# Second block of a two-block transformer kernel: the order of the input chunks, the convolution's taps and head 0's scores

## The reference, cut to what matters

```
fx, cqx, ckvx, krx, gx = split(modulate(rms_norm(x)) @ w_in[l])
q  = rms_norm(cqx, q_norm_g) @ w_uq                 # 8 heads, 64 + 32 rotated
kv = rms_norm(ckvx, kv_norm_g) @ w_ukv              # 8 heads, 64 keys + 64 values
attn = softmax((qn kn + rope(qr) rope(kr)) * scale) @ v      # keys: context and tokens
u = a * sigmoid(g)                                  # a, g: the halves of gx
u = conv(u, w_dw) + b_dw                            # depthwise, 31 taps along the tokens
y_c = silu(layer_norm(u)) @ w_pw2
y_f = Re(fft2(fx)) @ w_fourier
x = x + gate * (concat(y_f, attn, y_c) @ w_o)       # then a feed-forward part
```

## Time and profile before

| what | value |
|---|---|
| median of three runs | 3596.69 us |
| the profiled execution | 3599.15 us, span 3597.4 us |
| PE busy in the span | 3484.3 us (97%) |
| DVE busy | 1746.7 us (49%) |
| ACT busy | 1376.2 us (38%) |
| mean granted PE clock | 0.996 |

### The profile page before, as it was taken

The page is one execution under the profiler, slowest core; times in us unless marked ns, Lnnn a source line. Parts: engine busy times, 40 slices in busy tenths (PEclk is TensorE's granted clock), DMA queues, the critical chain, the costliest instruction groups (busy, mean ns, idle before and its releaser), DMA issues.

```text
span 3597.4 us, 46920 instructions
## 1 busy us (share of the span) xinstructions
PE 3484.3 (97%) x17777; PEld 2703.5 (75%) x17777; DVE 1746.7 (49%) x2536; ACT 1376.2 (38%) x2048; POOL 6.2 (0%) x13
## 2 busy tenths in 40 slices
PE   8999999999999989999999899899999999999999
PEld 5565788777775656887777776588888886579998
DVE  6674434443366754344333557543333356843334
ACT  5553323322245643233222334533323334443334
POOL 0000000000000000000000000000000000000000
PEclk9999999999999999999999999999999999999999
DMA  4121233555541212335565320022222222023332
GB/s 128 51 66 50 79 94 100 152 151 142 156 106 54 63 52 76 94 110 138 161 177 145 94 60 4 2 59 60 64 64 63 60 78 68 4 59 91 91 93 88
DMA packets 577230, 310.26 MB, mean 86 GB/s; under 512 B 28400, under 2 KB 569024, under 8 KB 577088
## 3 DMA queue, kind: packets, MB, share of 16 engines
q1 hardware_dynamic: 576816, 308.18, 30.3%
q10 hardware_dynamic: 272, 0.13, 0.0%
HBM read 297.26 MB, written 2.10 MB: 83 GB/s over the span
## 4 chain that ended last, share of the span: by engine, by line
PE 90%; DVE 4%; ACT 3%; issue 2%; DMA 1%; SPq 0%; DVEq 0%; ACTq 0%
PE ps L1129 14%; PE ps L1130 14%; PE ps L1131 14%; PE ps L1438 10%; PE ps L1440 10%; PE ps L1442 10%; PE ps L1319 2%; PE ps L1638 2%; PE ps L1288 2%; PE ps L1300 1%; PE ps L1213 1%; PE ps L1573 1%; PE ps L1316 1%; PE ps L1294 1%; DVE cacc L2963 1%
## 5 line engine op out<-in xcount | busy, mean ns | idle before, releaser
L1799 ACT ACTIVATE whi<-wraw 128x1024 fp32r<-128x1024 f32 x448 | 470.8, 1052 | 554.4 <-DMA wraw<-in_w_mlp 246.7
L1129 PE MATMUL ps<-uhi,whi 128*128 128x512 f32 (+1 forms) x1456 | 613.1, 421 | 12.4 <-DVE ulo L2454 5.3
L2437 DVE TENSOR_TENSOR wlo<-wraw,whi 128x1024 fp32r<-128x1024 f32 x448 | 545.9, 1219 | 106.6 <-ACT whi L1799 102.0
L1130 PE MATMUL ps<-ulo,whi 128*128 128x512 f32 (+1 forms) x1456 | 572.3, 393 | 0.0
L1131 PE MATMUL ps<-uhi,wlo 128*128 128x512 f32 (+1 forms) x1456 | 572.0, 393 | 0.0
L1129 PEld LDWEIGHTS ps<-uhi,whi 128*128 128x128 f32 x1456 | 274.0, 188 | 102.9 <-issue 38.5
L1130 PEld LDWEIGHTS ps<-ulo,whi 128*128 128x128 f32 x1456 | 274.4, 188 | 72.2 <-issue 16.3
L1131 PEld LDWEIGHTS ps<-uhi,wlo 128*128 128x128 f32 x1456 | 273.6, 188 | 65.2
L1438 PE MATMUL ps<-u2hi,whi 128*128 128x512 f32 (+1 forms) x1216 | 295.7, 320 | 3.6 <-DVE wlo L2437 2.4
L1438 PE MATMUL ps<-yhi,whi 128*128 128x512 f32 (+1 forms) x976 | 295.9, 353 | 0.0
L1440 PE MATMUL ps<-ylo,whi 128*128 128x512 f32 (+1 forms) x976 | 295.0, 353 | 0.0
(11 more groups left out here) (335 smaller groups left out, 4527.2 us busy)
## 6 DMA issues: line engine op xcount, KB each, us to landing
wraw<-in_w_in SPq DMA_DIRECT2D x128, 512.0 KB, 3.8
wraw<-in_w_mlp SPq DMA_DIRECT2D x128, 512.0 KB, 4.0
mod_raw<-in_w_mod SPq DMA_DIRECT2D x96, 512.0 KB, 5.2
wraw<-in_w_mlp_in SPq DMA_DIRECT2D x64, 512.0 KB, 4.3
wraw<-in_w_mlp_out SPq DMA_DIRECT2D x64, 512.0 KB, 3.9
wraw<-in_w_branch SPq DMA_DIRECT2D x16, 512.0 KB, 3.4
wraw<-in_w_out SPq DMA_DIRECT2D x16, 512.0 KB, 3.8
wraw<-in_w_o SPq DMA_DIRECT2D x16, 512.0 KB, 3.8
```

The lines of the kernel that those rows point to most:

```text
L1129: pe.matmul(bank, whs[:, i], x_hi[:, k], start=(i == 0), stop=False)
L1130: pe.matmul(bank, whs[:, i], x_lo[:, k], start=False, stop=False)
L1799: act.activation(whi[:, r], wraw[:, r], ACT.Copy).then_inc(w_hi, 1)
L2437: dve.tensor_tensor(wlo[:, r], wraw[:, r], whi[:, r].bitcast(F32), ALU.subtract).then_inc(w_split, 1)
```

## The change

Only the hand-written list ahead of the loop over heads changes, and with it the place of two rotations in SP's queue. The new list puts both conv and both conv_gate chunks in front of the q chunks. 30 of the 62 taps of the first layer and 19 of the second stand among the input chunks and head 0's first steps (13 and 10 before). The q norm comes behind the first fourier chunk, directly followed by head 0's queries. Head 0's scores alternate with the values and head 1's keys, and the second fourier chunk stands ahead of them all.

```diff
--- before.py
+++ after.py
@@ -354,18 +354,18 @@
     kv = Step("rank_norm", what="kv", tiles=1, width=ALL)
     q = Step("rank_norm", what="q", tiles=2, width=width)
     taps = [Step("tap", slot=t, tap=i) for t in range(2) for i in range(TAPS)]
-    shares = [4, 4, 2] if last else [5, 5, 3]
-    order = [chunk("kv", IN_KV), Step("rank_square", norm=kv), chunk("kr", IN_KR), kv, chunk("q", IN_Q), Step("key_rotate"),
-             chunk("q", IN_Q + P, 1), Step("rank_square", norm=q), chunk("conv", IN_CONV), q, Step("head_key", h=0),
-             Step("key_rest", h=0, width=ALL), chunk("conv_gate", IN_GATE), query(0), *taps[:shares[0]], chunk("conv", IN_CONV + P, 1), rotate(0),
-             *taps[shares[0]:sum(shares[:2])], chunk("conv_gate", IN_GATE + P, 1),
-             Step("query_round", h=0, width=width), query(1), *taps[sum(shares[:2]):sum(shares)], chunk("fourier", IN_FOURIER),
-             *scores(0, 0, 1, 2),
-             rotate(1), chunk("fourier", IN_FOURIER + P, 1), *scores(0, *range(3, a_units)),
-             Step("values", index=0), Step("head_key", h=1), Step("query_round", h=1, width=width),
-             Step("key_rest", h=1, width=ALL), Step("mla_column", h=0, width=width), Step("values", index=1), Step("values", index=2),
-             Step("mla_row", h=0, width=width)]
-    taps = taps[sum(shares):]
+    shares = [0, 4, 8, 12, 16, 18, 19] if last else [0, 6, 12, 18, 23, 27, 30]
+    early = [taps[lo:hi] for lo, hi in zip(shares, shares[1:])]
+    order = [chunk("kv", IN_KV), Step("rank_square", norm=kv), chunk("kr", IN_KR), kv, chunk("conv", IN_CONV),
+             Step("key_rotate"), chunk("conv_gate", IN_GATE), Step("head_key", h=0), Step("key_rest", h=0, width=ALL),
+             chunk("conv", IN_CONV + P, 1), *early[0], chunk("conv_gate", IN_GATE + P, 1), *early[1], chunk("q", IN_Q),
+             *early[2], chunk("q", IN_Q + P, 1), Step("rank_square", norm=q), *early[3], chunk("fourier", IN_FOURIER),
+             q, query(0), rotate(0), *early[4], chunk("fourier", IN_FOURIER + P, 1), Step("query_round", h=0, width=width),
+             query(1), *early[5], *scores(0, 0), Step("values", index=0), *scores(0, 1), rotate(1),
+             Step("values", index=1), *scores(0, 2), Step("head_key", h=1), *scores(0, 3), Step("key_rest", h=1, width=ALL),
+             Step("values", index=2), *scores(0, *range(4, a_units)), Step("query_round", h=1, width=width),
+             Step("mla_column", h=0, width=width), Step("mla_row", h=0, width=width)]
+    taps = taps[shares[-1]:]
     fill = {0: [Step("fourier_features", index=i) for i in range(2 if last else 3)],
             1: [Step("fourier_positions", index=0, width=width)], 2: [Step("fourier_positions", index=1, width=width)],
             3: [Step("fourier_map", index=t, width=width) for t in range(2)]}
@@ -1068,11 +1068,10 @@
                     for to, start in ((64, 80), (80, 64)):
                         sp.dma_start(sq2[to:to + 16, 1, 0:SEQ], sq2[start:start + 16, 0, 0:SEQ]).then_inc(mla_rot_in, 16)
 
-                rotation(rotations[0])
                 for j in range(HI_AHEAD):
                     column_chunk(s.out.chunk + j, a["w_o_2"][l], P * j)
-                    if j == 1:
-                        rotation(rotations[1])
+                    if j:
+                        rotation(rotations[j - 1])
                 sp.wait_ge(chunk_done, last_in + 1)
                 for i in range(2):
                     sp.dma_start(dft[:, i], a["dft_positions"][i].rearrange("(k p) c -> p k c", p=P)).then_inc(dft_in, 16)
```

## The result

The changed kernel takes 3619.99 us (median of 4 runs, 3616.01 to 3623.54), the kernel before beside it 3596.99 us: a ratio of 1.0058, 95% interval 1.0046 to 1.0070. It is slower by 23 us; the forecast was 3609.7 us with a range up to 3616. The profiled runs have spans of 3617.8 and 3597.4 us, 20.4 us apart.

The account below looks back on a forecast made before the run. PE was taken as nearly full, so new waits on it are paid in full. Entries +15.0, heads -5.0, clock +3.0 gave +13.0: 3612.1 us profiled, 2.5 less as median, 3609.7; range 3602 to 3616.

Parts of the forecast that it names:

- The entries' waits: Input chunks with head 0, both layers: PE waits for the norm and head 0's pieces add 7.65 and 7.35 us.
- Fewer taps in the heads: Heads behind the entries: taps that leave shorten PE's waits on DVE, -5.0 us; bounds nothing and -7.5.
- the column waits: First layer's heads: PE's waits for the column copy, 4.4 us before, shrink by 3.5.
- the maxima: First layer's heads: PE's waits for a maximum, 1.4 us before, shrink by 1.0.
- I take two of the four, rounded down to 3.0: Both entries: two of four long waits bring half clock at 1.7 us each, +3.0 us; bounds nothing and 6.8.
- all four waits: New PE waits above 2.4 us: 3.75 and 2.8 for the norm, 2.75 and 2.7 at the end of the entries.
- The column wait: End of head 0: the row of maxima waits behind copy, rounding, rest and column copy, 2.75 and 2.7 us.
- the norm's wait: First query product, directly behind the norm's sums, waits for root and scalings: 3.75 and 2.8 us.
- The step to the median: Whole kernel: the median of runs lies 2.5 us below the profiled execution, so 3612.1 becomes 3609.7 us.
- The clock stays low: Rival, chance 0.06: half clock from the norm to the first head, +24 us instead of +13.0, 3621 us.
- pass the waiting query product: Rival, chance 0.04: PE runs the second Fourier chunk while the query product waits, hiding the norm, 3584.1 us.
- the heads did not give 7.5: Rival, chance 0.17: heads give all 7.5 us, clock stays up, entry waits fall short by 2: +5.5, 3602.2 us.

Follow-up runs that it names:

- few_taps: Changed kernel with 13 and 10 taps under the input chunks instead of 30 and 19, the rest in the heads: 3623.13 us.
- filled_half: Changed kernel with products nobody reads put on PE into the three longest waits of each entry, sized to fit them: 3611.89 us, ratio 1.0034 to the kernel before.
- the second profile: Profile of the changed kernel run once more with no edit: 3620.04 us, ratio 1.0060 to the kernel before.

## Why the prediction was wrong

**The entries' waits: right, mechanism and size.** 15.0 was forecast, 15.9 came (+8.1 and +7.8). All that was read from durations and queue order held to 0.4 us a term.

**Fewer taps in the heads: right mechanism, 1.5 us too much.** -5.0 was forecast, -3.5 came. In the first layer the column waits gave 3.0 of the 3.5 and the maxima 0.9 of the 1.0, but a new wait of 0.36 us for cu and small ones took some back; the second layer's -0.5 was -0.1, as few_taps shows from the other side.

**The clock: this step failed.** It is the term "I take two of the four, rounded down to 3.0", with its bound "4 x 1.7 = 6.8". PE's busy time grew by 7.5 us in the four stretches; filled_half, which takes away the idling and not the waiting, gives 5 to 8 us back. Two things were wrong. In both profiles of the changed kernel all four waits were followed by half clock; none was spared because "work with gaps" follows. And the price of 1.7 us per wait was one case: the four cost 1.7, 3.2, 1.7 and 3.3 us in the first profile and 2.8, 3.2, 3.1 and 1.7 in the second. The trace of before had a second case 17 us behind the one that was read. Two PE rows and a window of it:

```profile
2318.99 0.50 PE L1617 MATMUL ps<-qhi,khi 97*128 97x512 f32 x1 [0.86 <-ACT wTx L2248]
...
2321.21 0.73 PE L1617 MATMUL ps<-qhi,khi 97*128 97x512 f32 x1 [1.26 <-ACT wTx L2248]
```

```profile
2321.30:2328.10 6.80, 6.80 (x16) 4.57 (x17) 1.31 (x2) 5.05 (x8) 0.00 (x0) 0.50 0.01 2
```

Two waits of 0.86 and 1.26 us, both far shorter than the 2.4 that the prediction counted from, are followed by 6.8 us of half clock, 3.4 lost. So neither the price of 1.7 nor the count of four was what the trace said.

Why one wait costs 1.7 and another 3.3 stays open. The column wait begins 2.2 us behind the end of a wait of 2.00, and the two short waits stand close together too, so waits at short distance may be priced together; but the norm's wait of the first layer, with no other wait of 0.8 us or more within 15 us, cost 2.8 in the second profile, and the column wait of the second layer 3.3 and then 1.7. No run here separates distance from chance. The Trainium skill (TensorE: Matmul & The Clock Gate, What's actually happening) holds that activity releases the slow clock; filled_half agrees, with 1.00 in the whole first entry. The prediction wrote that by this rule the sum would lie nearer its upper bound, and then took the lower half.

**The step to the median.** The forecast took off 2.5 us because the profiled run of before lay that far above the median shown. Later medians of the same kernel are 3598.6 to 3599.7, so most of that was chance: its mean granted clock lies between 0.993 and 0.997 from run to run, and its time goes with it (3606.45 us at 0.993, 3593.15 at 0.997). Profile to profile the forecast was +13.0 and the result +20.4; the rest of the 23 is this.

**The rivals.** "The clock stays low" named 3621, almost the measured time, but not by its mechanism: in the first layer the half clock ended 3.5 us behind the norm's wait, within the query product and before the second Fourier chunk began; in the second layer it took in 3.4 us of that chunk, not the whole. PE did not pass the waiting query product (3.76 us of nothing), and the heads did not give 7.5.

## What to carry to other kernels

Where PE is nearly always busy, price a new wait as its length plus half clock behind it: here 16 us of waits cost another 5 to 8. Which wait loses its cover can be read term by term from durations and queue order, and that part could be trusted here. For the half clock a single case in a trace is no price list: look at every stretch of it in the trace of before, and at what PE did ahead of each, before leaving a wait out as too short or taking a price. Before moving work out of one place, ask what it stands in front of in the other: the same taps made the column copy, the key rest, the query's rest or the first maximum late, wherever they stood.

## What was not expected of the hardware

Whether a wait of about 2 us is followed by half clock was chance here. Over the 14 profiles the same wait of 1.80 us (ahead of L1477, between the layers) was followed by it in 5, that of 2.31 us at the second layer's first norm in 7, that of 2.48 us on wTx in 9. Of 3.76 us it was in 5 of 5, of 2.80 us in 4 of 5, and of the column waits of 2.5 to 2.7 us, which follow other waits, in 8 of 8. The length alone does not order them: the pair of 0.86 and 1.26 us late in the first layer's heads, which the change leaves as it was, was followed by half clock in 14 of 14, with 1.7 to 3.4 us lost. The Trainium skill (TensorE: Matmul & The Clock Gate, What's actually happening) says that the number of slow products at the start of one kernel varies from run to run; the two profiles of the changed kernel agree for the middle of one, with 1.7 and 2.8 us lost behind the same norm wait.

Half clock does not cost its nominal price everywhere. Window of the changed kernel behind the wait of 1.80 us:

```profile
2953.00:2956.40 3.40, 3.40 (x9) 2.63 (x8) 3.37 (x7) 1.60 (x3) 0.00 (x0) 0.50 0.32 94
```

By busy time 1.7 us are lost there, but the way from the first layer's output product to the second layer's first norm is 630.0 us in all nine profiles without half clock there and 630.4 to 630.6 in the five with it: VectorE is busy for 3.37 of the 3.40 us, and sets the pace.
